# Transposes of a differential-attention layer: from matrix-engine transposes per tile to 32-partition block transposes over many tiles on VectorE

## The reference

```python
proj = u @ w_in                                   # [q | k | v | z]
logits = einsum(q_blk, k) * scale + rel_bias      # causal mask: NEG above the diagonal
p = softmax(logits)                               # two heads of a pair: p0, p1
a = p0 - lam * p1                                 # (queries, keys)
o = einsum('bhqs,bhsd->bhqd', a, v)
o = rms_norm(o, subln_g) * (1.0 - lam_init)
y = (o * silu(z)) @ w_out
out = layer_norm(alpha * h + y, ln_g, ln_b)
```

## Time and profile before

| | us |
|---|---|
| median of 3 runs | 968.7 |
| lowest of them | 968.24 |
| the profiled execution's own time | 968.76 |
| its span in the trace | 966.8 |
| TensorE busy | 953.4 (99%) |
| DVE busy | 463.9 (48%) |
| ACT busy | 319.0 (33%) |
| POOL busy | 63.1 (7%) |
| TensorE's mean granted clock | 0.996 of full speed |

### The profile page before, as it was taken

How to read it: one execution, slowest core, us unless ns; L and a number is a source line. 1 busy time by engine, 2 the same in 40 slices (tenths; PEclk the granted TensorE clock), 3 DMA queues, 4 the chain that set the end, 5 groups by cost and what they waited for, 6 DMA issues and landing times.

```text
span 966.8 us, 11791 instructions
## 1 busy us (share of the span) xinstructions
PE 953.4 (99%) x4432; PEld 797.0 (82%) x4432; DVE 463.9 (48%) x758; ACT 319.0 (33%) x572; POOL 63.1 (7%) x133
## 2 busy tenths in 40 slices
PE   8999999999999999999999999999999999999995
PEld 7888888888888888888888888888888878888884
DVE  4544723472347234723472347234723584424475
ACT  4423332333233323332333233323322453112211
POOL 2100100010001000100010001000100011000022
PEclk9999999999999999999999999999999999999998
DMA  8722242223222322242223222322232223542423
GB/s 294 273 87 88 88 136 87 88 87 136 87 87 87 136 87 87 87 136 87 87 87 136 87 87 87 136 87 87 87 108 87 87 87 112 193 152 87 153 98 119
DMA packets 33365, 108.60 MB, mean 112 GB/s; under 512 B 4272, under 2 KB 5296, under 8 KB 33088
## 3 DMA queue, kind: packets, MB, share of 16 engines
q1 hardware_dynamic: 28896, 94.65, 28.9%
q0 software_dynamic: 2336, 9.48, 2.8%
q10 hardware_dynamic: 2112, 4.19, 1.2%
HBM read 104.07 MB, written 9.48 MB: 117 GB/s over the span
## 4 chain that ended last, share of the span: by engine, by line
PE 96%; DVE 2%; DMA 1%; ACT 0%; SPq 0%; issue 0%; POOLq 0%; POOL 0%; ACTq 0%
PE proj L835 80%; PE att L835 15%; PE att L929 1%; PE att L954 1%; DMA big<-x_cols_dram 1%; DVE scratch L623 0%; DVE xg_split L768 0%; DVE w_split L788 0%; SPq L287 0%; POOLq L75 0%; POOL big L401 0%; DVE xg_split L597 0%; ACT xg_split L418 0%; ACT xg_split L543 0%; ACT big L581 0%
## 5 line engine op out<-in xcount | busy, mean ns | idle before, releaser
L835 PE MATMUL proj<-w_split,xg_split 128*128 128x512 f32 x1872 | 434.3, 390 | 0.0
L835 PEld LDWEIGHTS proj<-w_split,xg_split 128*128 128x128 f32 x1872 | 349.4, 188 | 71.4
L835 PE MATMUL proj<-xg_split,w_split 128*128 128x512 f32 x1536 | 360.1, 392 | 1.0 <-DVE w_split L726 0.8
L835 PEld LDWEIGHTS proj<-xg_split,w_split 128*128 128x128 f32 x1536 | 286.3, 188 | 60.1 <-DVE xg_split L597 1.6
L414 ACT ACTIVATE w_split<-w_raw 128x1024 fp32r<-128x1024 f32 x128 | 135.8, 1061 | 411.1 <-PE proj L835 403.7
L591 DVE TENSOR_TENSOR w_split<-w_raw,w_split 128x1024 fp32r<-128x1024 f32 x128 | 156.7, 1224 | 215.7 <-ACT w_split L414 214.1
L635 DVE CUSTOM_DVE_ANT_0 scratch<-att,bias 128x128 f32<-128x128 f32 (+3 forms) x64 | 28.9, 489 | 88.7 <-PE att L835 87.3
L835 PEld LDWEIGHTS att<-operands 128*128 128x128 f32 x432 | 64.0, 190 | 7.6 <-DVE operands L660 1.5
L835 PE MATMUL att<-operands 128*128 128x256 f32 (+3 forms) x432 | 69.2, 299 | 1.1 <-DVE scratch L670 1.1
L835 PE MATMUL att<-w_split,xg_split 128*128 128x512 f32 x288 | 66.1, 389 | 0.0
L835 PEld LDWEIGHTS att<-w_split,xg_split 128*128 128x128 f32 x288 | 54.1, 188 | 11.2
(11 more groups left out here) (76 smaller groups left out, 416.3 us busy)
## 6 DMA issues: line engine op xcount, KB each, us to landing
w_raw<-w_in_tiles_dram SPq DMA_DIRECT2D x126, 512.0 KB, 3.3
w_raw<-w_out_tiles_dram SPq DMA_DIRECT2D x32, 512.0 KB, 3.3
bias_by_distance<-bias_lines POOLq DMA_DIRECT2D x8, 640.0 KB, 6.5
bias<-bias_by_distance POOLq DMA_DIRECT2D x8, 512.0 KB, 5.2
x_res<-in_x_dram ACTq DMA_DIRECT2D x4, 1024.0 KB, 5.7
out_dram<-big SPq DMA_DIRECT2D x16, 256.0 KB, 2.7
big<-x_cols_dram SPq DMA_DIRECT2D x7, 512.0 KB, 8.7
scratch<-in_ln_g_dram SPq DMA_DIRECT2D x1, 1024.0 KB, 5.7
```

What stands on the lines that cost most here:

```text
L835: return nc.tensor.matmul(dst, lhsT, rhs, start=start, stop=stop, skip_group_check=True)
```

## The change

TensorE makes no transposes any more. On DVE a function `turn` covers a 128x128 transpose with sixteen block operations, each of which reads 32 partitions and writes 32 partitions; each operation runs over all tiles of a group at once. There are three groups in a pair: the six tiles of `t` 0 to 2 (`turn_a_early`, 32x6x32 elements an operation), the four of `t` 3 (`turn_a_late`, 32x4x32), and all eight of `gated` (`turn_gated`, 32x8x32). The turned tiles lie in SBUF `scratch` and no longer in PSUM. `a_rows` has a place for all ten tiles. The places of `scratch` are dealt out anew, which brings two waits on DVE: the first `logits_of` of a pair waits for the `g_copy` of the pair before, and the first `gate` waits for the turned tiles of `a`. In DVE's order `turn_a_early` stands in slot 13, `combine(3)` and `turn_a_late` in slot 14, `aT_split(0)` and `(1)` in slot 15, and `turn_gated` in step 5 of the next pair. On ACT `aT_split(0)` and `(1)` move from slot 13 to slot 14, and one `g_copy` of twice the size in step 6 takes the place of two.

```diff
+            def turn(dst, src):
+
+                for i in range(P // B):
+                    for j in range(P // B):
+                        last = nc.vector.transpose(dst[j * B:(j + 1) * B, ..., i * B:(i + 1) * B],
+                                                   src[i * B:(i + 1) * B, ..., j * B:(j + 1) * B])
+                return last
+
+            def turn_a_early(p):
+
+                dve.wait_ge(a_ready, p * ST + ST - 1)
+                if not (isinstance(p, int) and p == 0):
+                    dve.wait_ge(aT_ready, p * ST)
+                turn(aT_early, a_rows[:, 0:A_EARLY]).then_inc(aT_done, 1)
+
+            def turn_a_late(p):
+
+                dve.wait_ge(a_ready, p * ST + ST)
+                turn(aT_late, a_rows[:, A_EARLY:A_TILES]).then_inc(aT_done, 1)
+
+            def turn_gated(p):
+
+                dve.wait_ge(gated_ready, p * ST + ST)
+                turn(gT, gated_tiles).then_inc(nT_done, 1)
...
                 if j == 13:
+                    turn_a_early(p)
+                if j == 14:
+                    combine(p, 3)
+                    turn_a_late(p)
+                if j == 15:
                     aT_split(p, 0)
                     aT_split(p, 1)
-                if j == 14:
-                    combine(p, 3)
...
-                if not (isinstance(p, int) and p == 0 and t < 2):
-                    dve.wait_ge(aT_done, n - 2)
...
+                if j == 5:
+                    turn_gated(p)
...
-            def g_copy(p, i):
-
-                act.wait_ge(nT_done, 2 * p + i + 1)
+            def g_copy(p):
+
+                act.wait_ge(nT_done, p + 1)
                 for e in range(2):
-                    src = turned.rearrange("p (t e s) -> p e t s", t=2, e=2)[:, e]
-                    dst = g[:, bass.ds(p * 2 + e, 1), 2 * i * P:2 * (i + 1) * P]
-                    last = nc.scalar.activation(dst.rearrange("p k (t s) -> p (k t) s", t=2), src, ACT.Copy,
+                    dst = g[:, bass.ds(p * 2 + e, 1)]
+                    last = nc.scalar.activation(dst.rearrange("p k (t s) -> p (k t) s", t=ST), gT[:, :, e], ACT.Copy,
                                                 scale=sub_g[:, e:e + 1])
...
-                if j in (4, 6):
-                    g_copy(p, j // 2 - 2)
+                if j == 6:
+                    g_copy(p)
...
             def late_inserts(p, j):
                 if j < ST:
                     weigh_v(p, j)
-                if j < 2:
-                    turn_a(p, j + 2)
-                if j in (3, 5):
-                    turn_gated(p, j // 2 - 1)
...
             def own_inserts(p, j):
                 if 9 <= j < 13:
                     scores_of(p, j - 9)
-                if j == 12:
-                    turn_a(p, 0)
-                    turn_a(p, 1)
```

More of the change, by code:

```diff
@@ L57 @@
 LEAD = RING - 1
+B = 32
+A_TILES = ST * (ST + 1) // 2
+A_EARLY = A_TILES - ST
 NC = 512
@@ L103, in diff_layer @@
         logits = scratch[:, 0:1024].rearrange("p (h s) -> p h s", h=2)
[L104 to L109, removed]
+        aT_late = scratch[:, 0:ST * P].rearrange("p (n c) -> p n c", n=ST)
+        gT = scratch[:, 0:1024].rearrange("p (t e c) -> p t e c", t=ST, e=2)
+        silu_z = scratch[:, 1024:2048].rearrange("p (t e) -> p t e", t=ST)
+        a_rows = scratch[:, 2048:2048 + A_TILES * P].rearrange("p (n c) -> p n c", n=A_TILES)
+        gated = scratch[:, 2048:3072].rearrange("p (t e) -> p t e", t=ST)
+        gated_tiles = scratch[:, 2048:3072].rearrange("p (t e c) -> p t e c", t=ST, e=2)
+        aT_early = scratch[:, 3328:3328 + A_EARLY * P].rearrange("p (n c) -> p n c", n=A_EARLY)
+        lam_vecs = scratch[:, 1024:1024 + 4 * HD].rearrange("p (i n) -> p i n", i=4)
+        lam_prod = scratch[:, 1536:1536 + 2 * HD].rearrange("p (i n) -> p i n", i=2)
+        bias_line = scratch[0:16, 2048:2048 + BIAS_W]
         ln_g_all, ln_b_all = scratch[:, 0:D], scratch[:, D:2 * D]
@@ L143, in diff_layer @@
         scores = att[:, 0:2]
-        turned = att[:, 2]
         av = att[:, 3, 0:PW]
@@ L233, in chunk_part, with a_tiles @@
             return j // QK, j % QK
+        def a_tiles(t):
+            return slice(t * (t + 1) // 2, (t + 1) * (t + 2) // 2)
         def turned_a(t):
-            return turned[:, P:3 * P] if t == 1 else turned[:, 0:(t + 1) * P]
+            return aT_late if t == ST - 1 else aT_early[:, a_tiles(t)]
         def x_unit_of(k):
@@ L451, in aT_split @@
                     act.wait_ge(av_done, p * ST + t - 1)
-                act.wait_ge(aT_done, p * ST + max(t, 1) + 1)
-                nc.scalar.activation(aT[:, t % 2, 0, 0:(t + 1) * P], turned_a(t), ACT.Copy).then_inc(aT_hi, 1)
+                act.wait_ge(aT_done, 2 * p + (1 if t < ST - 1 else 2))
+                nc.scalar.activation(aT[:, t % 2, 0, 0:(t + 1) * P], turned_a(t).rearrange("p n c -> p (n c)"),
+                                     ACT.Copy).then_inc(aT_hi, 1)
             def norm(p, t):
@@ L538, in g_split_hi @@
                 if i == OQ - 1:
[L539 removed]
+                    act.wait_ge(g_ready, PAIRS)
                 else:
[L541 removed]
+                    act.wait_ge(g_ready, PAIRS - 1)
                 act.wait_ge(quarter_done, TOTAL)
@@ L669, in gate @@
                 dve.wait_ge(silu_ready, n)
+                if t == 0:
+                    dve.wait_ge(aT_done, 2 * p + 2)
                 nc.vector.scalar_tensor_tensor(gated[:, t], av, o_scale[:, t:t + 1], silu_z[:, t],
@@ L917, in scores_of @@
                 last.then_inc(scores_done, 1)
[L919 to L923, removed]
-                elif t > 1:
-                    pe.wait_ge(aT_ready, p * ST + t)
-                for kt in range(t + 1):
-                    src = slice(kt * P, (kt + 1) * P)
-                    dst = slice((kt + (t == 1)) * P, (kt + (t == 1) + 1) * P)
-                    last = nc.tensor.transpose(turned[:, dst], a_rows[:, t % 2, src], ident[:])
-                last.then_inc(aT_done, 1)
             def weigh_v(p, t):
@@ L944, in weigh_v @@
                 last.then_inc(av_done, 1)
-            def turn_gated(p, i):
-                pe.wait_ge(gated_ready, p * ST + 2 * i + 2)
-                if i == 0:
-                    pe.wait_ge(aT_ready, p * ST + ST)
-                else:
-                    pe.wait_ge(g_ready, 2 * p + 1)
-                for t in range(2):
-                    for e in range(2):
-                        last = nc.tensor.transpose(turned[:, (2 * t + e) * P:(2 * t + e + 1) * P],
-                                                   gated[:, 2 * i + t, e * P:(e + 1) * P], ident[:])
-                last.then_inc(nT_done, 1)
             def late_inserts(p, j):
```

19 lines of the change are left out of this document (11 added, 8 removed).

## The result

The changed kernel takes **990.9 us** (median of 4 runs, 989.17 to 991.45) against 968.5 for the kernel before: ratio 1.0229, 95% interval 1.0209 to 1.0249. The kernel before ran four times here: 968.24, 968.3 and 968.7 us, and one execution of 1961.02 us, which the ratio leaves out. The forecast was 979.5, in a range of 954 to 1004. The profiled execution took 991.09 us, its span is 989.2 against 966.8: +22.4 us.

The account below looks back on a forecast made before the run. TensorE, busy 99% of the span, was taken to bound the kernel. The terms -15.8 + 20.0 + 4.0 + 2.5 gave +10.7 on 968.8, so 979.5 us, in a range of 954 to 1004.

Parts of the forecast that it names:

- a dearer block transpose: DVE's block transposes priced up to the high end, 0.07 us more each: 990 to 1004 us; chance 0.17.
- within two per cent of the kernel before: Whole-kernel outcome between 949.3 and 988.1 us: chance 0.62, against slower 0.37 and faster 0.01.
- What is removed, 15.8 us: On TensorE, 144 transposes for `a` and `gated` at 0.11 us each disappear: 15.8 us less.
- The price of a block transpose: On DVE, 0.32, 0.39 and 0.46 us for 128, 192 and 256 elements without overlap; 151 us in all.
- The boundary step by step: At seven pair boundaries, `vz_tiles` ends at +19.2 against quarter 0 at +16.35: TensorE waits 2.9 us each, +20.0 us.
- The last boundary: At the output block's start, a +4.8 us wait, and the `gate(0)` wait 0.3 instead of 1.1: together +4.0 us.
- The last turn of `gated`: At the end, the last split of `g` comes at 13.4 where TensorE wants it at 10.9: +2.5 us.
- The clock: Rival: TensorE's clock falls at each boundary, 5.45 us each, 1018, or the last only, 985; clock or rate above 1004: 0.17.
- Later asks are met: After the boundary, DVE's weight splits and `turn_gated` come in time for TensorE; no further wait.
- the prediction's own signs of being wrong: No wait at quarter 0, operations over 0.5 us, a clock below 1.00 inside the program, or a wait elsewhere.

Follow-up runs that it names:

- experiment 1: The changed kernel with each group of sixteen block transposes replaced by one plain copy on DVE, the turning left out; 952.3 us, ratio 0.9832.
- experiment 7: The changed kernel with each block transpose written back to the 32 partitions it came from, moves across partition groups left out; 953.9 us, ratio 0.9849.
- experiment 3: The kernel before with one long reciprocal (790 columns) on DVE ahead of vz_tiles at the boundaries of pairs 0 to 6; 993.3 us, ratio 1.0251.
- experiment 6, second part: The changed kernel with each group of sixteen block transposes replaced by a plain copy and two reciprocals lasting as long together; 989.3 us, ratio 1.0205.
- experiment 2: The changed kernel with vz_tiles 0 and 1 put behind the tenth of sixteen late block transposes at the boundaries of pairs 0 to 6; 965.5 us, ratio 0.9969.
- experiment 4: The changed kernel with only slot 15's weight split and two aT_split put behind vz_tiles 0 and 1 at boundaries of pairs 0 to 6; 968.8 us, ratio 1.0005.
- experiment 5: The kernel before with a DVE reciprocal of 665 or 925 columns ahead of vz_tiles at seven boundaries; 984.7 us (ratio 1.0174) and 1004.2 us (1.0372).
- experiment 6 (first part): The changed kernel with fifteen more transposes of ident on TensorE behind quarter 5 of each pair; 1001.6 us (994.3 to 1003.4).

## Why the prediction was wrong

The side was right and the size was not: +10.7 us was forecast and +22.4 measured. The time lies inside the wide range of 954 to 1004, but in the band from 990 to 1004 that the prediction gave to a dearer block transpose, and the block transpose was not dearer; that the band was met is luck. The outcome that it held likeliest, within two per cent of the kernel before (0.62), did not come; slower had 0.37. By its own steps:

- **What is removed, 15.8 us.** Right within 0.6: 16.1 us in experiment 1, with a wait 0.3 us longer.
- **The price of a block transpose.** 0.32, 0.39 and 0.46 us against 0.32, 0.38 and 0.45 measured (303, 370 and 436 ns of length and 0.01). Right, and for the reason given: no overlap when the partition group changes (experiment 7). The 151 us of new DVE work came out as 142 busy.
- **The boundary step by step.** `turn_a_early` was to start 2.8 us behind T13, and the second `vz_tiles` move to end at +19.2 with a wait of 2.9. T13 is 379.4 in the profile after: 382.24 is +2.8, 398.3 is +18.9, the wait 2.57. Right; seven holes are 18.0 us where 20.0 stood.
- **The last boundary.** +4.8 and -0.8 were named; 4.57 and -1.1 came. Right.
- **The last turn of `gated`.** +2.5 named, 2.49 measured.
- **The clock.** This is the step that failed. The sum put nothing for it: the fall stood as a rival of its own, priced at a whole quarter (5.45 us a boundary, 1018), or at the last boundary alone (985). What was seen lies between: a fall at every boundary, with 3.4 us at the lower level and 1.7 us lost each time (6.8 and 2.3 at the last), 14.1 us in all. Without that term the measured parts give -15.8 - 1.1 + 18.0 + 4.6 + 2.5 = +8.2, 977. The rival's mechanism was right and three times too dear, and the forecast lacked it. Behind the opening, no row of before had a hole of more than 1.1 us with work on both sides. But the trace of before did bear on 2.9 us, in the window that the earlier trace rows leaves out:

```profile
959.00:961.00 2.00, 0.00 (x0) 0.00 (x0) 1.99 (x4) 0.81 (x1) 0.86 (x2) 0.68 0.00 0
```

The clock was 1.00 up to 959 and 0.50 from 961; a mean of 0.68 between them puts the fall near 959.7, 2.7 us behind the last product at 957.0. A wait of 2.9 us is longer than that, so part of the price belonged in the sum rather than none. A clock below 1.00 inside the program was among the prediction's own signs of being wrong, and TensorE's busy time fell by 1.7 us and not by about 16.

- **Later asks are met.** Right: no wait on a weight split and none on `scores_of`.

Why seven holes of seven lost the clock in the changed kernel and three of seven in experiment 3 is only half settled. It is not the block transposes (experiment 6, second part). It is not the length alone: the clock fell behind 2.2 to 2.3 us seven times of seven, behind 2.45 to 2.49 us at step 7 in two runs of four (experiment 2 and the second part of 6, but not the changed kernel or experiment 4), behind 2.58 us three times of seven and behind 3.42 us all but once. Executions of one program differ as well (994 to 1003 us in experiment 6). That the moment of the hole decides fits all of this but was not shown by itself, and the two differences that experiment 6 names are left; the run with a longer pair, made to show it, gave six falls and not three or four.

## What to carry to other kernels

Work moved off the engine that bounds the kernel is a gain only if the engine that takes it has the time just ahead of each thing the first one asks for; here a DVE 61% busy cost 40 us in one order and nothing in another. List what stands ahead of each hand-over on the receiving engine, and let long bundles of small operations be cut so that the hand-over goes between them. And price a hole on TensorE at its length plus what the clock takes: behind holes of 1.8 to 3.4 us that was 0.1 to 1.8 us more (2.7 once), behind 4.2 to 4.6 us it was 1.7 to 3.0. So two holes of 2.6 us are dearer than their sum says, and a cut of 1.7 us of work can be worth 3.

## What the runs showed of the hardware

- TensorE's granted clock fell to 0.50 behind some holes and not behind others of the same length. In the profiled executions:

| hole, us | falls | where |
|---|---|---|
| 0.4 to 1.1 | 0 of 20 | experiments 2 and 4 in the loop, `gate(0)` before and in 3 and 5, step 7 in 6 (first part) and 7 |
| 1.4 and 1.6 | 0 of 2 | experiments 1 and 7 |
| 1.8 | 1 of 7 | experiment 5 |
| 2.2 to 2.3 | 7 of 7 | experiment 6, second part |
| 2.5, at step 7 | 2 of 4 | changed kernel, experiments 2, 4 and 6 (second part) |
| 2.5 to 2.6 | 16 of 21 | changed kernel 7 of 7, experiment 6 (first part) 6 of 7, experiment 3 3 of 7 |
| 3.4 | 6 of 7 | experiment 5 |
| 4.2 to 4.6 | 5 of 5 | last boundary of the changed kernel, experiments 2, 4 and both parts of 6 |

- The fall is not tied to one moment of the hole. It came between 2.5 us before TensorE took up work again and 1.4 us behind that (in experiment 3, near 402.6 with the work begun at 401.68). The clock stayed down for 3.4 us, or for 6.8 us in five of the falls, all of which began 0.8 to 2.5 us before the work. The quarter behind it took 1.5 to 1.8 us more than the 5.6 without a hole, and 2.1 to 3.0 us more in those five.
- A float32 block transpose on DVE over 32 partitions takes 303, 370 and 436 ns for 128, 192 and 256 elements a partition, about 1.04 ns an element and 0.17 us of fixed part, 12 to 20 ns above a subtraction of the same size. The Trainium skill's 311 ns for 128x128 in bf16 ("VectorE: DVE Perf Modes", "The three transpose paths") is near it. With the partition group changing at each, the next one starts 0.01 us behind the end; with the group kept, sixteen of them take 0.09 us less each.
- In a stream of products a float32 transpose of a 128x128 tile costs TensorE 0.11 us, less than one of sixteen block operations for it (0.3 us); but one block operation serves up to eight tiles, so 144 transposes (15.8 us of TensorE) became 384 operations (142 us of DVE).
